# In the layer-norm feeds, GpSimd adds the mean row to every second k-tile

## The chip, the cores and the metric

The kernel runs on one core of a Trainium2 chip. The metric is device time in microseconds (us), the median of several runs. TensorE multiplies matrices, VectorE and ScalarE work element by element, GpSimd is a further elementwise engine, and SyncE issues the DMAs. All of them read and write SBUF; TensorE writes its results into PSUM banks, of which there are eight, each with a row of 512 float32 in each of 128 partitions.

## The reference, cut to what matters

The kernel computes a transformer-like model of three blocks over 512 tokens of 1024 features. What matters here is the layer norm and its place:

```
def layer_norm(t, g, b):
    mu = tf.mean(-1, keepdims=True)
    var = jnp.square(tf - mu).mean(-1, keepdims=True)
    return ((tf - mu) * lax.rsqrt(var + EPS) * g + b)

x = layer_norm(ALPHA * x + m[:, 2] * y, ...)
x = layer_norm(ALPHA * x + m[:, 5] * conv_glu_ffn(modulate(x, ...), *ffn, rows, GRID_W), ...)
u = silu(layer_norm(u, ln_g, ln_b))      # inside the conformer, ahead of u @ w2
```

Each of these results is the input of a matrix product.

## The kernel before, in words

Activations lie with the features in the partitions: a tensor of 1024 features by 512 tokens is `DT` = 8 k-tiles of 128 x 512 float32. A product over the features keeps its accuracy by splitting both operands into a rounded high part (type fp32r) and the low rest; `three_passes` (L245) then issues three matmuls, high by high, low by high and high by low, for each k-tile and output tile.

The kernel is a row of stages. Within a stage each engine runs its own list of instructions in order, and semaphores order the engines among each other; between two stages all engines meet. A stage that begins with a layer norm has a *feed*, an object of the class `LayerFeed` (L456). There are four: at the start of the first feed-forward block (tiles `ffn_x`), of the conformer's gate (`conf_x`), of the conformer's output product (`conf_in`), and of the second feed-forward block (`ffn_x` again). The mean times the inverse deviation, negated, is one row per token, spread over all partitions; so is the inverse deviation itself. In three feeds `closing` has left both in PSUM, the deviation in bank 6 and the mean in bank 7. In the `conf_in` feed both lie in SBUF (`stats`).

For k-tile k a feed does this:

- scale: VectorE multiplies `x[k]` by the row of inverse deviations (L481)
- center: VectorE adds the mean row (L472)
- form and high: ScalarE applies gain, bias and function twice, into `form`, a buffer of two tiles (L495), and into the high part (L497)
- low: VectorE subtracts the high part from `form` (L477)
- products: TensorE runs six matmuls on the k-tile (L248 to L250), three for each of two output tiles whose weights are already there.

VectorE's order is scale(k), center(k-1), low(k-2). ScalarE may form tile k only when low(k-2) is done, since `form` has two tiles. TensorE waits for low(k). While the feed begins, TensorE runs a few products on constants whose results nobody reads (`fill`, L256). Behind the feed each engine goes on in its list: ScalarE and VectorE split the next weights (L1048 and L1111, L1307 and L1367, L743 and L790 by stage), and SyncE fetches further weights when a slot has been split.

In these stages GpSimd only clears the borders of the convolution's buffer (L1015, L1246); in the `conf_in` stage it has nothing to do. `core.mean` is a row of 128 x 512 in SBUF which `closing` uses for a running sum, and which is free while a feed runs.

Of the kernel before, what the change touches and what calls it, by code (L numbers as in the profile page):

```python
# [11 lines left out]
ALU = mybir.AluOpType  # L12
ACT = mybir.ActivationFunctionType
# [4 lines left out]
DT = D // P  # L18
# [437 lines left out]
class LayerFeed:  # L456
# [3 lines left out]

    def __init__(self, core, x, parts, form, scale, bias, func=ACT.Identity, stats=None):
        self.rstd, self.mean = stats or (core.banks[6][:, :], core.banks[7][:, :])
        self.x, self.parts, self.form, self.scale, self.bias, self.func = x, parts, form, scale, bias, func

    names = ["scaled", "centered", "formed", "fed_high", "fed"]

    def dve(self, dve, scaled, centered, formed, fed_high, fed):
        x, form = self.x, self.form

        def center(k):  # L470
            dve.wait_ge(scaled, k + 1)
            dve.tensor_tensor(x[:, k, :], x[:, k, :], self.mean, ALU.add).then_inc(centered, 1)  # L472

        def low(k):
            dve.wait_ge(formed, k + 1)
            dve.wait_ge(fed_high, k + 1)
            dve.tensor_tensor(self.parts[1][:, k, :], form[:, k % 2, :], self.parts[0][:, k, :].bitcast(F32), ALU.subtract)\  # L477
               .then_inc(fed, 1)

        for k in range(DT):  # L480
            dve.tensor_tensor(x[:, k, :], x[:, k, :], self.rstd, ALU.mult).then_inc(scaled, 1)  # L481
            if k >= 1:
                center(k - 1)
            if k >= 2:
                low(k - 2)
        center(DT - 1)
        low(DT - 2)
        low(DT - 1)

    def act(self, act, scaled, centered, formed, fed_high, fed):  # L490
        for k in range(DT):
            act.wait_ge(centered, k + 1)
            if k >= 2:
                act.wait_ge(fed, k - 1)
            act.activation(self.form[:, k % 2, :], self.x[:, k, :], self.func, scale=self.scale(k), bias=self.bias(k))\  # L495
               .then_inc(formed, 1)
            act.activation(self.parts[0][:, k, :], self.x[:, k, :], self.func, scale=self.scale(k), bias=self.bias(k))\  # L497
               .then_inc(fed_high, 1)


class RootFeed:
# [6 lines left out]
    names = ["formed", "fed_high", "fed"]  # L508
# [22 lines left out]
class PlainFeed:  # L531
# [5 lines left out]
    names = ["fed_high", "fed"]  # L537
# [11 lines left out]
def closing(core, name, weights, acts, x, gate=None, center=True, eps=EPS, ahead=0, nxt=None, source=None, feed=None, rest=None, sq=None, lead=None,  # L549
# [27 lines left out]
    for t, k0, k1, prepared in bounds:  # L577
        if prepared:
            units.append((t, k0, k1, None))
        else:  # L580
# [7 lines left out]
    names = ["piece_in0", "piece_in1", "piece_high", "piece_low", "used", "taken", "r_done", "squared", "first_sum", "shift_done",  # L588
             "shifted", "body_sums", "last_sums", "counted", "var_done", "root_done", "inverted", "eps_in", "x_in",
             "x_ready", "next_in", "next_high", "summed_up", "squares_up"]  # L590
# [6 lines left out]
    with core.room(**rows) as (ring, shift, stat, eps_col, *own), \  # L597
            core.split_room(**{f"{name}_w": [P, slots - ready, per, P]}) as (own_w,), core.stage(*names) as (block, *sems):
        high, low = [[w_ready[n] for w_ready in (lead.ready if lead else ())] + [own_w[n][:, i] for i in range(slots - ready)]
                     for n in range(2)]  # L600
# [5 lines left out]
        feed_sems = extra[:len(feed.names)] if feed else []  # L606
# [6 lines left out]
        @block.sync  # L613
        def _(sp):
            def fetch(n):
                t, k0, k1 = pieces[n]
                if n >= 2 + ready:
                    sp.wait_ge(piece_low, n - 1 - ready)
                sp.dma_start(ring[:, n % 2, 0:k1 - k0], w[:, k0:k1, t * P:(t + 1) * P]).then_inc(piece_in[n % 2], 16)

            fetch(ready)
            fetch(ready + 1)
            if source is not None and not lead:
                sp.dma_start(x[:], source).then_inc(x_in, 16)
            for n in range(ready + 2, len(pieces)):
                fetch(n)
                if n == ready + 3 and lead:
                    sp.wait_ge(lead.fed_in(lead_sems), DT)
                    sp.dma_start(x[:], source).then_inc(x_in, 16)
                if n == ready + 3 and nxt is not None:  # L630
                    for slot in range(2):
                        sp.dma_start(core.pre_ring[:, slot], nxt[slot]).then_inc(next_in, 16)

        if lead:
            @block.gpsimd
# [255 lines left out]
class LastPair:  # L891


    names = ["value_in", "late_tapped0", "late_tapped1", "late_active", "late_products", "late_high", "late_low"]
# [66 lines left out]
def glu_ffn(core, name, w_up, gate_at, value_at, w_down, make_feed, x, renew, width, interior, taps, middle, conv_w, conv_b, func,  # L961
# [14 lines left out]
    with core.split_room(**{f"{name}_h": [P, FT, SEQ]}) as (h,), \  # L976
            core.room(**{f"{name}_pad": [P, 2, width], f"{name}_acc": [P, 2, SEQ], f"{name}_val": [P, 2, SEQ],
                         f"{name}_lit": [P, 2, SEQ]}) as (pad, acc, val, lit):
        with core.split_room(**{f"{name}_x": [P, DT, SEQ], f"{name}_w": [P, 2, DT, P]}) as (parts, (high, low)):
            feed = make_feed(parts, lit)  # L980
            names = ["slab_in0", "slab_in1", "high_done", "low_done", "tile_done", "banks_free", "bordered", "padded", "tapped0",
                     "tapped1", "active", "products", "h_high", "h_low", "slots_refilled", "next_in", "next_high"]
            with core.stage(*names, *feed.names) as (block, *sems):
                (slab_in0, slab_in1, high_done, low_done, tile_done, banks_free, bordered, padded, tapped0, tapped1, active,
                 products, h_high, h_low, slots_refilled, next_in, next_high, *feed_sems) = sems
                fed = feed_sems[-1]
# [11 lines left out]
                @block.sync  # L998
                def _(sp):
                    for u in range(2, 4):  # L1000
                        sp.dma_start(ring[:, u % 2], w[:, :, bass.ds(slab_at(0, u), P)]).then_inc(slab_in[u % 2], 16)
                    with sp.Fori(1, steps) as i:
                        for u in range(4):
                            feature = sp.snap(slab_at(i, u))
                            sp.wait_ge(low_done, 4 * i + u - 1)
                            sp.sem_inc(slots_refilled, 1)
                            sp.dma_start(ring[:, u % 2], w[:, :, bass.ds(feature, P)]).then_inc(slab_in[u % 2], 16)
                    for u in range(2):
                        sp.wait_ge(low_done, 4 * steps + u - 1)
                        sp.dma_start(ring[:, u], down[:, DT * u:DT * (u + 1), 0:P]).then_inc(next_in, 16)  # L1010

                @block.gpsimd
                def _(pool):
                    for j in range(2):
                        pool.memset(pad[:, j, :], 0.0).then_inc(bordered, 1)  # L1015

# [163 lines left out]
def conformer_gate(core, w1, w2, x, renew, make_feed, conv):  # L1180
# [24 lines left out]
    def theirs(j):  # L1205
# [3 lines left out]
    names = ["slab_in0", "slab_in1", "high_done", "low_done", "tile_done", "border", "banks_free", "gated", "begun",  # L1209
             "tapped", "diag_done", "pe_tapped", "added", "first_sum", "shift_done", "r_done", "squared", "mean_sum",  # L1210
             "summed", "mean_done", "square_done", "var_done", "root_done", "inverted", "eps_in", "next_in", "next_high"]
    with core.split_room(conf_x=[P, DT, SEQ], conf_w=[P, 2, DT, P]) as (parts, (high, low)), \
# [3 lines left out]
        with core.stage(*names, *feed.names) as (block, *sems):  # L1216
# [17 lines left out]
            @block.sync  # L1234
            def _(sp):
                for s in range(2, 2 * DT):
                    if s >= 4:
                        sp.wait_ge(low_done, s - 1)
                    sp.dma_start(ring[:, s % 2], slab(s)).then_inc(slab_in[s % 2], 16)
                for u in range(2):  # L1240
                    sp.wait_ge(low_done, 2 * DT)
                    sp.dma_start(ring[:, u], out[:, :, u * P:(u + 1) * P]).then_inc(next_in, 16)

            @block.gpsimd
            def _(pool):
                pool.memset(pad[:], 0.0).then_inc(border, 1)  # L1246

            @block.tensor
# [329 lines left out]
class Folds:  # L1578
# [8 lines left out]
    def pool(self, pool, scaled, folded):  # L1587
        core, mods = self.core, self.mods
        for n, (layer, part) in enumerate(((0, 3), (1, 0), (1, 3))):
            shift, scale = [mods[layer][:, (part + e) * DT:(part + e + 1) * DT, 0] for e in range(2)]  # L1590
            gain, bias = [core.cols_sb[:, COL_AT[name] + n:COL_AT[name] + 4 * DT:4] for name in ("post_ln_g", "post_ln_b")]
            pool.tensor_tensor(core.fold_sb[:, 0, n, :], gain, scale, ALU.mult).then_inc(folded, 1)
            pool.tensor_tensor(core.fold_sb[:, 1, n, :], bias, scale, ALU.mult).then_inc(scaled, 1)
            pool.tensor_scalar(core.fold_sb[:, 2, n, :], gain, ALPHA, None, ALU.mult).then_inc(folded, 1)
            pool.tensor_scalar(core.fold_sb[:, 3, n, :], bias, ALPHA, None, ALU.mult).then_inc(folded, 1)
            pool.wait_ge(scaled, n + 1)
            pool.tensor_tensor(core.fold_sb[:, 1, n, :], core.fold_sb[:, 1, n, :], shift, ALU.add).then_inc(folded, 1)
        at = COL_AT["conf_b2"]
        out_gate = mods[1][:, 2 * DT:3 * DT, 0]
        pool.tensor_tensor(self.gated_bias[:, :], out_gate, core.cols_sb[:, at:at + DT], ALU.mult).then_inc(scaled, 1)  # L1600
        pool.wait_ge(scaled, 4)
        pool.wait_ge(folded, 12)
        pool.tensor_tensor(core.fold_sb[:, 3, 1, :], core.fold_sb[:, 3, 1, :], self.gated_bias[:, :], ALU.add).then_inc(folded, 1)
# [2729 lines left out]
```

## Time and profile before

| what | value |
|---|---|
| median of 3 runs | 2852.64 us (2845.04 to 2854.54) |
| the profiled execution's own time | 2843.07 us |
| its span in the profile | 2841.3 us |
| TensorE busy | 2636.8 us (93% of the span) |
| VectorE busy | 1650.8 us (58%) |
| ScalarE busy | 1088.6 us (38%) |
| GpSimd busy | 162.6 us (6%) |

The profile records one execution. Its own time is 1.8 us longer than the span, and 9.6 us (0.34%) below the median of the runs. A busy TensorE counts each matmul from its start to its modelled end, so consecutive ones overlap a little. In all rows, PE is TensorE, PEld its weight load, DVE VectorE, ACT ScalarE, POOL GpSimd and SP SyncE; times in a timeline are counted from the start of the span.

### The profile page before, as it was taken

How to read it: one execution, taken by the hardware profiler on the slowest of the kernel's cores; microseconds unless marked ns; L12 is line 12 of the kernel's file. 1: busy time of each engine (PE TensorE's matmuls, PEld its weight loads, DVE VectorE, ACT ScalarE, POOL GpSimd, SP SyncE). 2: the span in 40 equal slices, each digit the busy share in tenths (PEclk: the TensorE clock that was granted, in tenths of full speed). 3: DMA queues.
4: the chain of work that ended last, by engine and by line, in shares of the span. 5: the costliest groups of instructions: out<-in, count | busy, mean ns of one | idle time of the engine just before them, and what ended most of it. 6: DMA issues, size and time to landing. Idle time of an engine off the chain costs nothing. (4 is left out here: it accounts for less than half of the span.)

```text
span 2841.3 us, 41630 instructions
## 1 busy us (share of the span) xinstructions
PE 2636.8 (93%) x16068; PEld 2026.0 (71%) x16068; DVE 1650.8 (58%) x2601; ACT 1088.6 (38%) x1798; POOL 162.6 (6%) x170
## 2 busy tenths in 40 slices
PE   6978899988889999999997899999899998999998
PEld 3743588776668788877663688878578866788886
DVE  3436412267766588743898688853664577544432
ACT  3441210146563455422523365532321154355521
POOL 0005300013222000000000000000000000000000
PEclk9989999999999999999998999999999999999999
DMA  8734312211114133241120233342332001333232
GB/s 299 242 115 145 122 45 67 59 37 41 43 44 132 53 103 92 78 133 46 45 58 16 60 104 96 96 113 65 92 100 67 3 10 30 83 102 96 81 110 69
DMA packets 382116, 240.93 MB, mean 85 GB/s; under 512 B 7825, under 2 KB 353809, under 8 KB 381969
## 3 DMA queue, kind: packets, MB, share of 16 engines
q1 hardware_dynamic: 381968, 238.89, 28.7%
q8 instruction: 102, 1.67, 0.3%
q14 instruction: 46, 0.37, 0.0%
HBM read 236.24 MB, written 2.10 MB: 84 GB/s over the span
## 5 line engine op out<-in xcount | busy, mean ns | idle before, releaser
L1149 DVE SCALAR_TENSOR_TENSOR ffn_acc<-ffn_pad,cols_sb,ffn_acc 128x512 f32<-128x512 f32 x380 | 264.0, 749 | 32.7 <-ACT ffn_acc L1076 32.7
L248 PE MATMUL bank<-ffn_x_high,pre_high 128*128 128x512 f32 x528 | 210.9, 399 | 4.9 <-DVE ffn_x_low L477 3.3
L250 PE MATMUL bank<-ffn_x_high,pre_low 128*128 128x512 f32 x528 | 209.0, 396 | 0.0
L249 PE MATMUL bank<-ffn_x_low,pre_high 128*128 128x512 f32 x528 | 208.9, 396 | 0.0
L248 PE MATMUL bank<-ffn_x_high,ffn_w_high 128*128 128x512 f32 x528 | 205.5, 389 | 0.0
L250 PE MATMUL bank<-ffn_x_high,ffn_w_low 128*128 128x512 f32 x528 | 205.5, 389 | 0.0
L249 PE MATMUL bank<-ffn_x_low,ffn_w_high 128*128 128x512 f32 x528 | 205.4, 389 | 0.0
L248 PE MATMUL bank<-ffn_h_high,ffn_down_w_high 128*128 128x512 f32 x480 | 190.5, 397 | 0.7 <-DVE ffn_h_low L944 0.7
L249 PE MATMUL bank<-ffn_h_low,ffn_down_w_high 128*128 128x512 f32 x480 | 189.6, 395 | 0.0
L250 PE MATMUL bank<-ffn_h_high,ffn_down_w_low 128*128 128x512 f32 x480 | 188.6, 393 | 0.0
L743 ACT ACTIVATE ffn_down_w_high<-ffn_down_ring 128x1408 fp32r<-128x1408 f32 (+1 forms) x45 | 60.5, 1345 | 211.1 <-PE bank L250 176.9
L790 DVE TENSOR_TENSOR ffn_down_w_low<-ffn_down_ring,ffn_down_w_high 128x1408 fp32r<-128x1408 f32 (+1 forms) x45 | 71.2, 1581 | 111.2 <-ACT ffn_down_w_high L743 111.2
L1372 DVE SCALAR_TENSOR_TENSOR conf_u<-conf_pad,cols_sb,conf_u 128x512 f32<-128x512 f32 x162 | 121.8, 752 | 16.9 <-ACT conf_u L1339 11.7
L1111 DVE TENSOR_TENSOR pre_low<-pre_ring,pre_high 128x1024 fp32r<-128x1024 f32 x60 | 73.4, 1224 | 97.9 <-ACT pre_high L1048 97.2
L248 PEld LDWEIGHTS bank<-ffn_x_high,pre_high 128*128 128x128 f32 x528 | 99.2, 188 | 36.0 <-DVE ffn_x_low L477 12.4
L250 PEld LDWEIGHTS bank<-ffn_x_high,pre_low 128*128 128x128 f32 x528 | 99.2, 188 | 24.3
L249 PEld LDWEIGHTS bank<-ffn_x_low,pre_high 128*128 128x128 f32 x528 | 99.3, 188 | 23.5
L248 PEld LDWEIGHTS bank<-ffn_x_high,ffn_w_high 128*128 128x128 f32 x528 | 99.1, 188 | 20.8 <-DVE ffn_w_low L1111 0.2
L249 PEld LDWEIGHTS bank<-ffn_x_low,ffn_w_high 128*128 128x128 f32 x528 | 99.1, 188 | 20.7
L250 PEld LDWEIGHTS bank<-ffn_x_high,ffn_w_low 128*128 128x128 f32 x528 | 99.1, 188 | 20.6
L1111 DVE TENSOR_TENSOR ffn_w_low<-pre_ring,ffn_w_high 128x1024 fp32r<-128x1024 f32 x66 | 80.5, 1223 | 47.6 <-ACT ffn_w_high L1048 47.6
L248 PEld LDWEIGHTS bank<-ffn_h_high,ffn_down_w_high 128*128 128x128 f32 x480 | 90.2, 188 | 23.4 <-DVE ffn_h_low L944 1.5
(731 smaller groups left out, 6207.8 us busy)
## 6 DMA issues: line engine op xcount, KB each, us to landing
ada_ring<-in_ada_w SPq DMA_DIRECT2D x48, 1024.0 KB, 7.0
pre_ring<-in_ffn_w_up SPq DMA_DIRECT2D x88, 512.0 KB, 3.9
pre_ring<-in_ffn_w_in SPq DMA_DIRECT2D x44, 512.0 KB, 3.9
ffn_down_ring<-in_ffn_w_down SPq DMA_DIRECT2D x28, 704.0 KB, 4.7
pj_ring<-in_w_in SPq DMA_DIRECT2D x24, 512.0 KB, 3.9
ffn_down_ring<-in_ffn_w_out SPq DMA_DIRECT2D x14, 704.0 KB, 4.3
pre_ring<-in_conf_w SPq DMA_DIRECT2D x18, 512.0 KB, 5.0
f_ring<-in_mix_w_in SPq DMA_DIRECT2D x32, 256.0 KB, 3.2
```

Source lines behind the costliest of these rows:

```text
L248: pe.matmul(bank, weights[0], acts[0], start=start, stop=False)
L249: pe.matmul(bank, weights[0], acts[1], start=False, stop=False)
L250: return pe.matmul(bank, weights[1], acts[0], start=False, stop=stop)
L743: act.activation(high[n % slots][:, 0:k1 - k0], ring[:, n % 2, 0:k1 - k0], ACT.Copy).then_inc(piece_high, 1)
L790: dve.tensor_tensor(low[n % slots][:, 0:k1 - k0], ring[:, n % 2, 0:k1 - k0], high[n % slots][:, 0:k1 - k0].bitcast(F32), ALU.subtract).the ...
L1111: dve.tensor_tensor(slot(u)[1], ring[:, u % 2], slot(u)[0].bitcast(F32), ALU.subtract).then_inc(low_done, 1)
L1149: dve.scalar_tensor_tensor(out=dst, in0=src, scalar=conv_w(2 * i + j, n), in1=dst, op0=ALU.mult, op1=ALU.add).then_inc(tapped[j], 1)
L1372: dve.scalar_tensor_tensor(out=conv[:, j, :], in0=pad[:, j % pads, n:n + SEQ], scalar=core.col("conf_dw_w", j, n), in1=conv[:, j, :], op0= ...
```

## The change

The centering of the odd k-tiles goes from VectorE to GpSimd. GpSimd cannot read the mean row in its PSUM bank, so ScalarE first copies it into `core.mean`; in the `conf_in` feed, where the row is in SBUF, only the semaphore is raised. VectorE centers the even tiles with the SBUF row too. VectorE's order becomes scale(k), scale(k+1), center(k), low(k-2), low(k-1) for k = 0, 2, 4, 6.

```
+    def pool(self, pool, scaled, mean_in, centered, pool_centered, formed, fed_high, fed):
+        pool.wait_ge(mean_in, 1)
+        for k in range(1, DT, 2):
+            pool.wait_ge(scaled, k + 1)
+            pool.tensor_tensor(self.x[:, k, :], self.x[:, k, :], self.mean_sb[:, :], ALU.add).then_inc(pool_centered, 1)
...
         def center(k):
+            if k == 0:
+                dve.wait_ge(mean_in, 1)
             dve.wait_ge(scaled, k + 1)
-            dve.tensor_tensor(x[:, k, :], x[:, k, :], self.mean, ALU.add).then_inc(centered, 1)
+            dve.tensor_tensor(x[:, k, :], x[:, k, :], self.mean_sb[:, :], ALU.add).then_inc(centered, 1)
...
-        for k in range(DT):
-            dve.tensor_tensor(x[:, k, :], x[:, k, :], self.rstd, ALU.mult).then_inc(scaled, 1)
-            if k >= 1:
-                center(k - 1)
-            if k >= 2:
+        for k in range(0, DT, 2):
+            scale(k)
+            scale(k + 1)
+            center(k)
+            if k:
                 low(k - 2)
-        center(DT - 1)
+                low(k - 1)
         low(DT - 2)
         low(DT - 1)
...
+        if self.own_mean is None:
+            act.activation(self.mean_sb[:, :], self.mean, ACT.Copy).then_inc(mean_in, 1)
+        else:
+            act.sem_inc(mean_in, 1)
         for k in range(DT):
-            act.wait_ge(centered, k + 1)
+            act.wait_ge(pool_centered if self.by_pool(k) else centered, k // 2 + 1)
```

In the stages, GpSimd's list gets `feed.pool(pool, *feed_sems)` ahead of the clearing of the borders (L1015, L1246), and in `closing` with a centered feed it gets a list with this alone.

## Rows read from the trace of the kernel before

**Rows 1.** Windows, conf_x and conf_in: busy PE, PEld, DVE, ACT, POOL; PEclk; DMA.

```profile
1340.80:1358.90 18.10, 15.64 (x55) 9.52 (x55) 16.15 (x27) 14.30 (x20) 1.46 (x1) 1.00 0.22 59
1549.40:1567.50 18.10, 15.34 (x52) 10.20 (x52) 16.11 (x27) 15.14 (x19) 0.00 (x0) 0.91 0.22 58
```

**Rows 2.** Timeline (start, duration, instruction, count, [idle <-releaser]), VectorE, conf_x feed.

```profile
1340.97 1.29 DVE L481 TENSOR_TENSOR x_sb<-x_sb,bank 128x512 f32<-128x512 f32 x2
...
1344.52 0.69 DVE L477 TENSOR_TENSOR conf_x_low<-conf_sq,conf_x_high 128x512 fp32r<-128x512 f32 x1 [0.47 <-ACT conf_x_high L497]
...
1348.12 0.69 DVE L477 TENSOR_TENSOR conf_x_low<-conf_sq,conf_x_high 128x512 fp32r<-128x512 f32 x1
...
1356.67 0.69 DVE L477 TENSOR_TENSOR conf_x_low<-conf_sq,conf_x_high 128x512 fp32r<-128x512 f32 x1 [0.72 <-ACT conf_x_high L497]
```

**Rows 3.** Timeline of ScalarE in the conf_x feed and behind it.

```profile
1342.89 0.81 ACT L495 ACTIVATE conf_sq<-x_sb,fold_sb 128x512 f32<-128x512 f32 x1 [5.34 <-DVE x_sb L472]
1343.61 0.80 ACT L497 ACTIVATE conf_x_high<-x_sb,fold_sb 128x512 fp32r<-128x512 f32 x1
...
1355.77 0.80 ACT L497 ACTIVATE conf_x_high<-x_sb,fold_sb 128x512 fp32r<-128x512 f32 x1
...
1368.65 0.81 ACT L1339 ACTIVATE conf_u<-conf_pad,cols_sb 128x512 f32<-128x512 f32 x1
```

**Rows 4.** Timeline of TensorE in the conf_x feed, up to the next tile.

```profile
1340.84 2.81 PE L256 MATMUL bank<-const_sb 128*128 128x512 f32 x6 [0.98 <-PEq L226]
...
1345.26 0.50 PE L248 MATMUL bank<-conf_x_high,pre_high 128*128 128x512 f32 x1 [1.61 <-DVE conf_x_low L477]
...
1357.50 0.41 PE L248 MATMUL bank<-conf_x_high,pre_high 128*128 128x512 f32 x1
...
1358.89 0.44 PE L248 MATMUL bank<-conf_x_high,conf_w_high 128*128 128x512 f32 x1
```

**Rows 5.** Timelines of the two ffn_x feeds: VectorE's first, TensorE in the last k-tile.

```profile
955.79 1.28 DVE L481 TENSOR_TENSOR x_sb<-x_sb,bank 128x512 f32<-128x512 f32 x2 [3.01 <-PEq L226]
...
972.58 0.50 PE L248 MATMUL bank<-ffn_x_high,pre_high 128*128 128x512 f32 x1
...
1620.56 1.28 DVE L481 TENSOR_TENSOR x_sb<-x_sb,bank 128x512 f32<-128x512 f32 x2 [2.99 <-PEq L226]
...
1637.10 0.40 PE L248 MATMUL bank<-ffn_x_high,pre_high 128*128 128x512 f32 x1
```

**Rows 6.** Timeline of the conf_in feed and what follows it.

```profile
1549.56 1.29 DVE L481 TENSOR_TENSOR conf_u<-conf_u,rstd 128x512 f32<-128x512 f32 x2
...
1565.32 0.69 DVE L477 TENSOR_TENSOR conf_in_low<-conf_form,conf_in_high 128x512 fp32r<-128x512 f32 x1 [0.72 <-ACT conf_in_high L497]
...
1567.45 1.51 SPq L619 DMA_DIRECT2D conf_out_ring<-in_conf_w  x2
...
1571.67 1.06 ACT L743 ACTIVATE conf_out_w_high<-conf_out_ring 128x1024 fp32r<-128x1024 f32 x1 [4.55 <-DMA conf_out_ring<-in_conf_w]
```

**Rows 7.** Timelines of GpSimd and VectorE in an earlier stage, from 844.9 us.

```profile
844.98 1.30 POOL L3022 TENSOR_TENSOR o_hg<-o_hg,o_gates 128x512 f32<-128x512 f32 x1 [35.53 <-ACT br_o_sq L3055]
...
845.46 1.37 DVE L3076 TENSOR_TENSOR y_low<-x_sb,y_high 128x512 fp32r<-128x512 f32 x1 [1.55 <-ACT y_high L3053]
...
846.24 1.74 POOL L3022 TENSOR_TENSOR o_hg<-o_hg,o_gates 128x512 f32<-128x512 f32 x1
...
846.75 1.78 DVE L3076 TENSOR_TENSOR y_low<-x_sb,y_high 128x512 fp32r<-128x512 f32 x1
```

**Rows 8.** Timelines of VectorE and GpSimd from 225 us.

```profile
225.23 2.48 DVE L2184 TENSOR_TENSOR xbc<-xbc,bank 128x512 f32<-128x512 f32 x4
...
226.13 1.90 POOL L2010 TENSOR_TENSOR ssd_xd<-x_tok,share 128x1024 f32<-128x1024 f32 x1
```

**Rows 9.** Groups by form, ScalarE (xcount | busy us, mean ns | idle before).

```profile
L1089 ACT ACTIVATE ffn_val<-bank 128x512 f32<-128x512 f32 x63 | 37.7, 599 | 155.5 <-PE bank L250 155.5
```

**Rows 10.** Timeline of TensorE in the conf_in feed, a matmul at the lower clock.

```profile
1556.70 0.63 PE L250 MATMUL bank<-conf_in_high,pre_low 128*128 128x512 f32 x1
```

More of the change, by code:

```diff
@@ L462, in __init__, with by_pool, dve, scale @@
         self.rstd, self.mean = stats or (core.banks[6][:, :], core.banks[7][:, :])
+        self.own_mean, self.mean_sb = stats, core.mean
         self.x, self.parts, self.form, self.scale, self.bias, self.func = x, parts, form, scale, bias, func
-    names = ["scaled", "centered", "formed", "fed_high", "fed"]
-    def dve(self, dve, scaled, centered, formed, fed_high, fed):
+    names = ["scaled", "mean_in", "centered", "pool_centered", "formed", "fed_high", "fed"]
+    def by_pool(self, k):
+        return k % 2 == 1
+    def pool(self, pool, scaled, mean_in, centered, pool_centered, formed, fed_high, fed):
[3 more added lines that the diff above has]
+            pool.tensor_tensor(self.x[:, k, :], self.x[:, k, :], self.mean_sb[:, :], ALU.add).then_inc(pool_centered, 1)
+    def dve(self, dve, scaled, mean_in, centered, pool_centered, formed, fed_high, fed):
         x, form = self.x, self.form
+        def scale(k):
+            dve.tensor_tensor(x[:, k, :], x[:, k, :], self.rstd, ALU.mult).then_inc(scaled, 1)
         def center(k):
+            if k == 0:
+                dve.wait_ge(mean_in, 1)
             dve.wait_ge(scaled, k + 1)
-            dve.tensor_tensor(x[:, k, :], x[:, k, :], self.mean, ALU.add).then_inc(centered, 1)
+            dve.tensor_tensor(x[:, k, :], x[:, k, :], self.mean_sb[:, :], ALU.add).then_inc(centered, 1)
         def low(k):
@@ L478, in low, with act @@
                .then_inc(fed, 1)
-        for k in range(DT):
-            dve.tensor_tensor(x[:, k, :], x[:, k, :], self.rstd, ALU.mult).then_inc(scaled, 1)
-            if k >= 1:
-                center(k - 1)
-            if k >= 2:
+        for k in range(0, DT, 2):
[3 more added lines that the diff above has]
+            if k:
                 low(k - 2)
-        center(DT - 1)
+                low(k - 1)
         low(DT - 2)
         low(DT - 1)
-    def act(self, act, scaled, centered, formed, fed_high, fed):
+    def act(self, act, scaled, mean_in, centered, pool_centered, formed, fed_high, fed):
+        if self.own_mean is None:
+            act.activation(self.mean_sb[:, :], self.mean, ACT.Copy).then_inc(mean_in, 1)
+        else:
+            act.sem_inc(mean_in, 1)
         for k in range(DT):
-            act.wait_ge(centered, k + 1)
+            act.wait_ge(pool_centered if self.by_pool(k) else centered, k // 2 + 1)
             if k >= 2:
@@ L632, in _ @@
                         sp.dma_start(core.pre_ring[:, slot], nxt[slot]).then_inc(next_in, 16)
+        if feed and center:
+            @block.gpsimd
+            def _(pool):
+                feed.pool(pool, *feed_sems)
         if lead:
@@ L1013, in _ @@
                 def _(pool):
+                    if renew is not None:
+                        feed.pool(pool, *feed_sems)
                     for j in range(2):
@@ L1245, in _ @@
             def _(pool):
+                feed.pool(pool, *feed_sems)
                 pool.memset(pad[:], 0.0).then_inc(border, 1)
```

## The prediction

> **What bounds the kernel now.** I read the busy shares first: TensorE is busy for 93% of the span and GpSimd for 6%, so GpSimd has room and only what TensorE waits for counts. The windows over the feeds come next [rows 1]: in 18.1 us of each, VectorE is busy for 16.1 us, ScalarE for 14.3 and 15.1, TensorE for 15.6 and 15.3 with its overlapping ends and its fills. Then the timelines tell who waits for whom. In the conf_x feed VectorE starts at 1340.97 [rows 2], and I count from there. Two scales take 1.29 us, so starts are 0.60 apart and one operation lasts 0.69. low(0) starts at 3.55, low(2) at 7.15: 1.80 us per k-tile, three operations of VectorE back to back. ScalarE begins to form at 1.92, its starts are 0.72 apart, and the last high ends at 15.60 [rows 3]. TensorE's fills are over at 2.68; its first product waits 1.61 us for low(0) and starts at 4.29, and the last k-tile's first product starts at 16.53 [rows 4]. Its six matmuls take 1.39 us, since the next product begins at 1358.89 [rows 4]; I use 1.40. So VectorE's 1.80 sets the pace, ScalarE's 1.43 and TensorE's 1.40 would be next. The feed is a fill of the pipeline: what it loses is lost for good, as long as the stage behind it has no slack. The ffn_x feeds have the same pattern, with the last k-tile's product at 16.79 and 16.54 after VectorE's start [rows 5]; the last low of conf_in ends at 16.45 [rows 6].
>
> **What is removed and what it would be worth.** Each feed takes 4 of 24 operations from VectorE. At 0.60 that is 2.40 us, 9.6 us in all. This holds only if VectorE's other operations keep their duration while GpSimd works.
>
> **What GpSimd does to VectorE.** The earlier stage has the same pair of operations side by side [rows 7]. GpSimd's first add runs alone in 1.30 us and ends at 846.28. VectorE's subtraction of two SBUF tiles starts at 845.46 and takes 1.37 instead of 0.69: it ends at 846.83, 0.55 after GpSimd's. GpSimd's next, started at 846.24, ends at 847.98, 1.15 after VectorE's. VectorE's next ends at 848.53, again 0.55 after. They alternate, each held until the other is through. An operation of VectorE with one input in PSUM is not held: four took 2.48 us in all, 0.68 each, although GpSimd ran a two-input operation through the last two [rows 8]. So I take from rows 7: GpSimd 1.30 alone, its end 1.14 after VectorE's where VectorE was first, VectorE's end 0.55 after GpSimd's where GpSimd was first. Scales out of PSUM run free; centers and lows, both now with two SBUF inputs, are held. The bounds are no hold at all and, above, this alternation.
>
> The Trainium skill says the same of the mechanism (SBUF — State Buffer, "SBUF: two separate sides"): the pair of ports that VectorE and GpSimd share is taken for a whole instruction, by whoever starts first, against a VectorE operation with two SBUF inputs. By its words a held operation would then need its whole 0.69 us, 1.99 in place of the 1.85 of the rows; the sum below would be near 7 us. The trace has 0.55, not 0.69, and I go by the trace.
>
> **The new order, step by step (three feeds with PSUM rows).** Times are from VectorE's start.
> - The copy of the mean row is priced at 0.60 like an eviction of this shape out of PSUM [rows 9]; ScalarE is idle for over 5 us before its first form [rows 3]. VectorE needs the row at 1.20. Cost 0. Without that cover it would be 0.6 per feed, 1.8.
> - scale(0) 0.00, scale(1) 0.60 to 1.29, center(0) 1.20 to 1.89. GpSimd could start on tile 1 at 1.33, is held by center(0), and ends at 3.03.
> - scale(2) 1.80, scale(3) 2.40 to 3.09, center(2) 3.00 to 3.69. GpSimd's tile 3 is held again and ends at 4.83.
> - low(0) could start at 3.60 (ScalarE's high(0) ends at 3.44). It is the loser now: it ends at 4.83 + 0.55 = 5.37, before 4.24. low(1) ends at 5.97.
> - The pair then repeats: scale, scale, center (3 x 0.60), a held low (1.77 less an overlap of 0.08), a free low (0.60): 4.09 us for two k-tiles, where before it was 3.60. low(2) ends at 9.46, low(4) at 13.55, low(5) at 14.15.
> - Tail. ScalarE's form(6) waits for low(4) as before for its buffer: form and high of 6 and 7 start 0.71 apart from 13.61, high(7) ends at 16.54, low(7) at 17.33. Before, 15.60 and 16.39: +0.95 on ScalarE and VectorE.
> - TensorE: first product at 5.42; from low(4) on it is the bound, four k-tiles of 1.40 behind 13.60: the last one's first product at 17.80.
>
> The same steps laid on the old order give 4.27 for the first product, 16.42 for the last k-tile's and 15.59 for the last high; the trace has 4.29, 16.53 and 15.60, so the method holds to 0.1 us.
>
> **Each feed.** In the ffn stages TensorE goes on without a pause, so its delay counts: 17.80 against 16.79 and 16.54 [rows 5], +1.0 and +1.3. In the conformer's gate the next thing is ScalarE's own list, through diagonals, sigmoid and renewal to conf_u at 1368.65, which VectorE's taps wait for [rows 3]: +0.95. In conf_in the row of deviations is in SBUF as well, so scale(2) is held by GpSimd: it ends at 3.57 instead of 2.49, and everything behind is 1.09 later. low(7) ends at 18.42 against 16.45: +2.0. What follows is VectorE's split of the first piece, which releases SyncE's next fetch (1567.45), which ScalarE waits for until 1571.67 [rows 6]; the delay goes through whole. Sum: 1.0 + 0.95 + 2.0 + 1.3 = +5.3 us.
>
> Border clearing moves behind GpSimd's four adds, to about 13 us after the start; it is wanted behind the feed, 7 us later. Cost 0 without a hold from GpSimd's clearing on VectorE's last lows; with one, one low would be later by at most the clearing's 1.46 us in conf_x [rows 1], and by less in the ffn feeds, where it is cut in two.
>
> **Rivals.**
> - *No hold in these stages.* The rows that show the hold [rows 7] are of an earlier stage; no feed has one yet, since GpSimd reads nothing there now. Then low(4) comes early enough that the ring of two forms and ScalarE set the pace: by the same steps high(7) would end at 14.03 and the last k-tile's product start at 15.3. Against the same steps on the old order that is -1.1 for each ffn feed and -1.6 for each of the others: -5.4, 2837.7 on the profiled execution, 2847.2 on the median. The full 9.6 (2843.0) would need ScalarE and TensorE to have no limit of their own; they have 1.43 and 1.40 per k-tile.
> - *TensorE's clock falls in the feeds.* This is the slower side. TensorE's idle time ahead of the first product grows from 1.61 to 2.7 us [rows 4], and by 2.2 us in conf_in. In conf_in the granted clock is already 0.91 over the window [rows 1]: for a part of it TensorE ran at 1.2 GHz instead of 2.4, a matmul 0.63 us instead of 0.40 [rows 10]. 0.09 of 18.1 us is 1.6 us of work, which is what such a stretch costs where TensorE is the bound. If it lies on the first two k-tiles, the gap ahead of low(2) (8.22 to 9.51) takes most of it up. One that is not covered in each of four feeds would give +6.4 more: 2864. It decides (over 0.3%) from three uncovered stretches on.
> - *The hold is real but falls less often.* GpSimd may start a little later than I take, and low(0) win against tile 3. This saves up to 1.1 per feed once: about +1 to +3, 2854 to 2856.
>
> **How the numbers follow.** The profiled execution took 2843.07 us; +5.3 makes 2848.4. The median of the runs is 9.6 us above it, and I add the same to it: 2852.64 + 5.3 = 2858. A change of 0.3% is 8.6 us, about what a measurement of this kernel can tell from none. Chances: the alternation as worked out, 0.55; held less often, 0.20; no hold, 0.08 (-0.19%, inside the 0.3%); the full gain of VectorE's time, 0.03; clock stretches or further waits, 0.14. The cases up to +8.6 us hold most of it: faster 0.05, same 0.81, slower 0.14. The range runs from no hold, 2847, to the alternation with four uncovered clock stretches and a little more, 2866.
>
> **What would show it.** GpSimd has four adds of about 1.7 us in each feed; low(0), low(2) and low(4) last about 1.77 us, low(1) and low(3) 0.69; scales out of PSUM stay at 0.68; low(2) to low(4) is 4.1 us; TensorE's first product moves to 5.4. Wrong if lows of 0.69 us lie beside GpSimd's adds, or if the feeds in ffn end earlier than 16.5. The prediction also falls if the stages behind the feeds give the delay back.

## The result, and the profile after

The changed kernel took 2860.74 us in the median of 20 runs (2852.06 to 2873.29), the kernel before 2851.86 us (20 runs, 2844.76 to 2856.05). The ratio is 1.0031 (95% interval 1.0022 to 1.0040): slower by 8.9 us, at the edge of the 0.3%. The forecast was 2858.0, which is +5.3 us. The profiled execution of the changed kernel took 2857.86 us and has a span of 2855.7 us.

The windows over conf_x (up to the next tile's first product) and conf_in answer to [rows 1]. Columns are those of [rows 1].

```profile
1352.30:1371.60 19.30, 15.71 (x55) 11.21 (x56) 17.25 (x22) 14.98 (x23) 7.96 (x5) 0.91 0.20 55
1561.50:1580.10 18.60, 14.50 (x45) 9.89 (x46) 16.64 (x21) 13.89 (x19) 6.55 (x4) 0.72 0.21 57
```

In conf_x the window has grown from 18.1 to 19.3 us. VectorE runs 22 instructions instead of 27 (four centers went to GpSimd, and a clearing of 0.06 us lies just outside the window) and is busy for 17.25 us instead of 16.15: fewer operations, more time. GpSimd's 7.96 us contain 1.46 of clearing. The granted clock is 0.91, where it was 1.00. The timeline of VectorE in this feed shows the longer operations (columns as in [rows 2]).

```profile
1352.32 1.28 DVE L481 TENSOR_TENSOR x_sb<-x_sb,bank 128x512 f32<-128x512 f32 x2
1353.52 0.68 DVE L487 TENSOR_TENSOR x_sb<-x_sb,mean 128x512 f32<-128x512 f32 x1
...
1355.92 2.36 DVE L492 TENSOR_TENSOR conf_x_low<-conf_sq,conf_x_high 128x512 fp32r<-128x512 f32 x2
...
1360.01 2.37 DVE L492 TENSOR_TENSOR conf_x_low<-conf_sq,conf_x_high 128x512 fp32r<-128x512 f32 x2
...
1364.10 2.37 DVE L492 TENSOR_TENSOR conf_x_low<-conf_sq,conf_x_high 128x512 fp32r<-128x512 f32 x2
...
1369.00 0.69 DVE L492 TENSOR_TENSOR conf_x_low<-conf_sq,conf_x_high 128x512 fp32r<-128x512 f32 x1 [0.72 <-ACT conf_x_high L516]
```

Two lows in a row take 2.36 us where two free operations take 1.28. The same view with a narrow window has the two of the first pair one by one:

```profile
1355.92 1.76 DVE L492 TENSOR_TENSOR conf_x_low<-conf_sq,conf_x_high 128x512 fp32r<-128x512 f32 x1
1357.61 0.68 DVE L492 TENSOR_TENSOR conf_x_low<-conf_sq,conf_x_high 128x512 fp32r<-128x512 f32 x1
```

All of the hold is in the first. GpSimd's timeline in the same feed tells what held it: the second of its first two adds ends at 1353.76 + 3.38 = 1357.14, and the low at 1357.68, 0.54 behind it.

```profile
1353.76 3.38 POOL L475 TENSOR_TENSOR x_sb<-x_sb,mean 128x512 f32<-128x512 f32 x2 [373.39 <-DVE x_sb L481]
1359.56 1.66 POOL L475 TENSOR_TENSOR x_sb<-x_sb,mean 128x512 f32<-128x512 f32 x1 [2.42 <-DVE x_sb L481]
1363.65 1.67 POOL L475 TENSOR_TENSOR x_sb<-x_sb,mean 128x512 f32<-128x512 f32 x1 [2.43 <-DVE x_sb L481]
1365.25 1.46 POOL L1273 MEMSET conf_pad<- 128x1626 f32 x1
```

TensorE's timeline there answers to [rows 4]: its first product waits 2.73 us instead of 1.61, and starts 5.42 us after VectorE's first operation instead of 4.29. It runs at the lower clock (0.63 us a matmul) until 1361.26 and at full clock from there on. It reaches the third k-tile at 1362.17, after low(2) has ended (1361.77), so there it waits no more; it still waits 0.86 us for low(4).

```profile
1357.74 0.74 PE L248 MATMUL bank<-conf_x_high,pre_high 128*128 128x512 f32 x1 [2.73 <-DVE conf_x_low L492]
1358.28 0.63 PE L249 MATMUL bank<-conf_x_low,pre_high 128*128 128x512 f32 x1
...
1365.92 0.50 PE L248 MATMUL bank<-conf_x_high,pre_high 128*128 128x512 f32 x1 [0.86 <-DVE conf_x_low L492]
...
1371.49 0.39 PE L248 MATMUL bank<-conf_x_high,conf_w_high 128*128 128x512 f32 x1
```

In conf_in, VectorE's timeline has one more hold, ahead of the first low. The row of deviations lies in SBUF, and scale(2) and scale(3) take 2.36 us together; the last low ends at 1580.03, 18.5 after the start, against 16.4 [rows 6].

```profile
1563.37 2.36 DVE L481 TENSOR_TENSOR conf_u<-conf_u,rstd 128x512 f32<-128x512 f32 x2
...
1566.26 2.35 DVE L492 TENSOR_TENSOR conf_in_low<-conf_form,conf_in_high 128x512 fp32r<-128x512 f32 x2
...
1579.34 0.69 DVE L492 TENSOR_TENSOR conf_in_low<-conf_form,conf_in_high 128x512 fp32r<-128x512 f32 x1 [0.72 <-ACT conf_in_high L516]
```

**Where the time went in the profiled executions.** Both traces hold the same instructions outside the feeds, so the same instruction can be looked up in both. The table has how much later each landmark lies in the changed kernel, in us.

| landmark | before | later by | added since the line above |
|---|---|---|---|
| first scale of the first ffn feed | 955.79 | 10.40 | |
| weight split behind it | 979.9 | 11.39 | +1.0 (forecast +1.0) |
| first scale of conf_x | 1340.97 | 11.35 | |
| first weight split behind it | 1358.7 | 12.33 | +0.98 (forecast +0.95) |
| first scale of conf_in | 1549.56 | 12.00 | -0.3 |
| splits behind it | 1586.9 | 14.13 | +2.13 (forecast +2.0) |
| first scale of the second ffn feed | 1620.56 | 14.14 | |
| weight splits some 60 us behind it | 1686.8 | 15.50 | +1.36 (forecast +1.3) |
| last normalization of that block | 1998.2 | 16.19 | +0.7 |
| beginning of the next stage | 2010.7 | 14.70 | -1.5 |
| own time of the execution | 2843.07 | 14.79 | +0.1 |

The four feeds cost 1.0 + 1.0 + 2.1 + 1.4 = 5.5 us, and nothing behind them gives it back: the offset of 15.50 stays the same to 0.02 us for 180 us. What lies outside them is small and of both signs; the -1.5 is explained under experiments 9 and 10, the +0.7 and -0.3 are not. The 10.4 us ahead of the first feed are not the change's. The instructions there are the same; 7.9 of them come from one stretch in which TensorE had the lower clock, seen in the windows 775 to 795, changed kernel first and kernel before second:

```profile
775.00:795.00 20.00, 20.00 (x166) 16.79 (x167) 4.89 (x10) 10.82 (x32) 0.00 (x0) 0.57 0.05 14
```

```profile
775.00:795.00 20.00, 18.35 (x207) 16.48 (x202) 7.34 (x20) 13.74 (x36) 0.00 (x0) 0.91 0.11 29
```

Experiments 3, 4, 6, 7, 9, 10 and 11 have this stretch too and 1, 2, 5 and 8 have not, whatever their feeds; it is scatter, and the profiled execution of before, at 2843.07 us, was faster than any of the kernel's 101 measured runs.

### The profile page after: what moved, and what is told of

It reads as the page before. It is cut to its first block and busy times, and to the rows that moved or that the text cites. A ratio compares the mean times of both kernels' runs of the same rounds, so it can differ in the third digit from the quotient of the medians.

```text
span 2855.7 us, 41642 instructions
## 1 busy us (share of the span) xinstructions
PE 2645.2 (93%) x16068; PEld 2037.5 (71%) x16068; DVE 1653.9 (58%) x2585; ACT 1089.8 (38%) x1801; POOL 188.2 (7%) x186
## 3 DMA queue, kind: packets, MB, share of 16 engines
q8 instruction: 102, 1.67, 0.3%
```

## The experiments

Each diff is against the changed kernel. Times of feeds are counted from VectorE's first operation; "next tile" is the first product of the next output tile, which lay at 18.31 (ffn), 17.92 (conf_x) and 17.95 (second ffn) before and lies at 19.33, 19.17 and 19.32 in the changed kernel.

**1. The new order, with VectorE adding the row to all tiles.** The mean row still comes from SBUF.

```diff
-        for k in range(1, DT, 2):          # GpSimd
+        for k in ():
...
             center(k)
+            center(k + 1)
...
-            act.wait_ge(pool_centered if self.by_pool(k) else centered, k // 2 + 1)
+            act.wait_ge(centered, k + 1)
```

> The changed kernel with VectorE's new order and the copied row, but with the odd tiles centered by VectorE, too, so GpSimd adds nothing. Theory (the cost of the change is the hold between GpSimd and VectorE): no low lasts longer than 0.69 us; counted from VectorE's first scale, the lows 0, 2, 4 start at 4.8, 8.4, 12.0, the last high ends at 15.7 and the last k-tile's products end at 18.3 in all four feeds; with the conf_in feed ending 2.0 us earlier than in the changed kernel. In all -5 us against the changed kernel and +1 against the kernel before, ratio to before 1.0004. Rival (the new order or the SBUF row costs the time, not GpSimd): ends near 17.3 us for the last low as in the changed kernel, ratio 1.003.

Measured: 2850.03 us, ratio 0.9995 (0.9980 to 1.0010). VectorE's timeline has two lows in 1.29 us throughout, although both inputs are in SBUF:

```profile
1350.22 1.29 DVE L492 TENSOR_TENSOR conf_x_low<-conf_sq,conf_x_high 128x512 fp32r<-128x512 f32 x2
1353.82 1.29 DVE L492 TENSOR_TENSOR conf_x_low<-conf_sq,conf_x_high 128x512 fp32r<-128x512 f32 x2
```

high(7) ends at 15.72, low(7) at 16.52, the next tile starts at 18.46, 18.33 and 18.47. So neither the copy, nor the SBUF row, nor the order costs more than 0.15 to 0.5 us per feed; what costs is GpSimd's work.

**2. GpSimd with one input.** GpSimd multiplies the odd tiles by 1.0 instead of adding the row, so the mean is left out of them.

```diff
-            pool.tensor_tensor(self.x[:, k, :], self.x[:, k, :], self.mean_sb[:, :], ALU.add).then_inc(pool_centered, 1)
+            pool.tensor_scalar(self.x[:, k, :], self.x[:, k, :], 1.0, None, ALU.mult).then_inc(pool_centered, 1)
```

> The changed kernel, but GpSimd multiplies its tiles by 1.0 (one input from SBUF) in place of adding the mean row (two inputs); this leaves the mean out of the odd tiles. GpSimd's operation should take about as long, near 1.5 us. Theory (the hold falls on two-input operations of both engines): the lows last 0.69 us, start at 3.60, 4.95, 7.35, the last high ends at 14.0 and the last low at 14.8 after the first scale; ratio to before 0.998 (-5 us). Rival 1 (any GpSimd operation on SBUF holds VectorE's two-input ones): lows 0, 2, 4 last about 2 us and the last low ends at 17.5 or later; ratio 1.003. Rival 2 (the changed kernel's time comes from lower clocks of TensorE, not from the feeds): feeds shorter, but ratio still 1.002 or more.

Measured: 2849.69 us, ratio 0.9992 (0.9979 to 1.0004). low(7) ends at 15.70: earlier than with two inputs (17.38), later than without any hold (14.8 expected). Neither of the two expected times is met, and the timelines of GpSimd and VectorE say why:

```profile
959.57 3.58 POOL L475 TENSOR_SCALAR x_sb<-x_sb 128x512 f32<-128x512 f32 x2 [73.42 <-DVE x_sb L481]
965.04 1.87 POOL L475 TENSOR_SCALAR x_sb<-x_sb 128x512 f32<-128x512 f32 x1 [1.89 <-DVE x_sb L481]
```

```profile
961.72 1.09 DVE L492 TENSOR_TENSOR ffn_x_low<-ffn_lit,ffn_x_high 128x512 fp32r<-128x512 f32 x1
963.07 0.69 DVE L492 TENSOR_TENSOR ffn_x_low<-ffn_lit,ffn_x_high 128x512 fp32r<-128x512 f32 x1 [0.26 <-ACT ffn_x_high L516]
```

GpSimd's one-input operation delays low(0) by 0.40 us instead of 1.07, and low(0) ends at 962.81, while GpSimd works on to 963.15. So this is not the alternation of [rows 7], in which one operation waits for the end of the other. Without the second input most of the hold is gone, and a smaller delay is left, whose mechanism these runs don't show. The edit also puts another and longer instruction in the place of the add, so it is not shown that the number of inputs alone makes the difference.

**3. VectorE centers with the PSUM row.** Only GpSimd uses the copy.

```diff
-            dve.tensor_tensor(x[:, k, :], x[:, k, :], self.mean_sb[:, :], ALU.add).then_inc(centered, 1)
+            dve.tensor_tensor(x[:, k, :], x[:, k, :], self.mean, ALU.add).then_inc(centered, 1)
```

> The changed kernel, but VectorE's centers of the even tiles read the mean row in its PSUM bank; GpSimd's read the copy. Theory (only VectorE operations with two SBUF inputs and GpSimd's two-input ones hold each other): the centers no longer hold GpSimd, whose first add lasts 1.30 instead of 1.69; lows 0, 2, 4 last 1.37 instead of 1.77, the pair takes 3.7 us in place of 4.1; in the three feeds with PSUM rows the last high ends at 15.4 and the last low at 16.2, the last products at 18.1. conf_in is unchanged. In all -3.4 us against the changed kernel. Rival (VectorE is held with PSUM operands as well): no change in the feeds, 17.3.

A single execution, 2859.19 us, which gives no ratio. GpSimd's and VectorE's timelines in conf_x:

```profile
1351.37 1.28 POOL L475 TENSOR_TENSOR x_sb<-x_sb,mean 128x512 f32<-128x512 f32 x1 [373.29 <-DVE x_sb L481]
1353.10 1.27 POOL L475 TENSOR_TENSOR x_sb<-x_sb,mean 128x512 f32<-128x512 f32 x1 [0.44 <-DVE x_sb L481]
```

```profile
1353.53 1.38 DVE L492 TENSOR_TENSOR conf_x_low<-conf_sq,conf_x_high 128x512 fp32r<-128x512 f32 x1
```

GpSimd, which no center holds any more, takes its 1.28 us instead of 1.58 to 1.67; low(0) takes 1.38 instead of 1.76, and ends 0.54 after GpSimd's add (1354.91 against 1354.37). high(7) ends at 15.51, low(7) at 16.31. The alternation is thus a matter of where operands lie: of VectorE's three kinds of operation, only those with two inputs in SBUF take part. conf_in, where both rows are in SBUF in either case, stays as in the changed kernel: its last low ends at 18.48.

**4. The old order with GpSimd.** scale(k), center(k-1) for odd k, low(k-2).

```diff
-        for k in range(0, DT, 2):
+        for k in range(DT):
             scale(k)
-            scale(k + 1)
-            center(k)
-            if k:
+            if k % 2:
+                center(k - 1)
+            if k >= 2:
                 low(k - 2)
-                low(k - 1)
```

> The change with the order of the kernel before: scale(k), center(k-1) where VectorE has it, low(k-2). Theory: low(0) is no longer late (3.54 us), but each odd low is held (1.77 us), the pair takes 4.1 us and the last low ends at 17.6, the last products at 19.5, 0.3 us later than with the new order. Rival (low(0)'s lateness of 1.2 us is what the new order costs): the last low ends near 16.4.

A single execution, 2866.24 us. Now the odd lows take 1.77 us, low(0) is free at 3.55, and low(7) ends at 17.72; the next tile starts at 19.68. The hold follows whichever low meets GpSimd. In the three feeds with PSUM rows the order of the change is the better one by 0.35 to 0.42 us. In conf_in it is the worse one: there the last low ends at 17.76 in the old order and at 18.48 in the new one. In both orders scale(2) is held there. In the old one it ends just as low(0) can start (3.56); in the new one low(0) meets GpSimd's next add as well and starts at 4.70.

**5. More fills.** Three more products on constants ahead of each feed's first product, so that TensorE idles less; one of three such edits is shown.

```diff
-                    fill(pe, core, core.banks[4], 3)
+                    fill(pe, core, core.banks[4], 6 if renew is not None else 3)
```

> The changed kernel with more products on constants ahead of the feeds' first product: 6 fills instead of 3 in the two ffn stages and the conformer's gate, 5 instead of 2 in conf_in, so TensorE's idle time ahead of the first product falls from 2.7 us to under 0.3 in three feeds. Theory (the time of the change is the held lows; the clock's falls in the feeds lie on gaps and cost nothing): the stretches of the lower clock that begin 5 to 7 us after the first scale go away, the feeds' ends stay (last low 17.4, next tile 19.3), and the ratio to before stays at 1.003 (1.002 to 1.004). Rival (the lower clock is what brings the measured +8.9 us above the +5.3 of the feeds): ratio 1.0015 or less.

Measured: 2858.95 us, ratio 1.0025 (1.0012 to 1.0038). The granted clock over the first ffn feed and conf_x is 1.00, and the feeds end where they did (next tile at 19.32, 19.22 and 19.34).

```profile
961.50:980.80 19.30, 17.05 (x60) 10.96 (x60) 17.28 (x22) 14.99 (x21) 7.74 (x6) 1.00 0.20 55
1347.40:1366.70 19.30, 17.02 (x61) 11.08 (x62) 17.23 (x23) 14.97 (x22) 7.97 (x5) 1.00 0.20 55
```

So the lower clock in the changed kernel's feeds costs nothing: the gaps ahead of low(2) and low(4) take it up. conf_in agrees: the changed kernel has 10.2 us of the lower clock there, this one 3.4, and the last low ends at 18.48 and 18.47. The granted clock over whole runs says the same: its mean is 0.971 in the kernel before, 0.969 in the changed kernel and 0.971 again with the fills, while the mean time is 2859.2 us (changed, all runs) and 2858.2 us (fills). The limit of this is seen in experiment 6, where the stretch in the first feed lasted 6.8 us: the next tile started at 19.51 instead of 19.33.

**6. conf_in as before,** the other three feeds as changed.

```diff
     def by_pool(self, k):
-        return k % 2 == 1
+        return k % 2 == 1 and self.own_mean is None
...
```

The rest of the edit gives conf_in its old order back.

> The changed kernel with the conf_in feed as before the change (its own order, all centers on VectorE). Theory: that feed is back at a last low ending at 16.4, the time from its first scale to that of the second ffn feed is 71.0 us instead of 73.1, and the other three feeds stay at 17.4. Rival (the stage behind conf_in would have absorbed it): that time stays within 0.5 us of the changed kernel's 73.1.

A single execution, 2859.72 us. low(7) of conf_in ends at 16.46, and from conf_in's first scale to that of the next feed it is 70.75 us, against 73.14 in the changed kernel and 71.00 before. The other feeds stay at 17.4. The delay of conf_in, 2.0 us in the feed, does go through whole: 2.1 us against before between these two marks, 2.4 against this run.

**7. GpSimd for two tiles, where no low waits.** GpSimd takes tiles 2 and 5 alone, VectorE centers the others from PSUM, and VectorE's order is written out so that no low has to wait for GpSimd; conf_in is left to VectorE, in the order of experiment 8.

```diff
+    def pool_tiles(self):
+        return (2, 5) if self.own_mean is None else ()
...
+        "S0 S1 C0 S2 C1 S3 S4 L0 C3 L1 S5 L2 C4 S6 L3 C6 L4 S7 L5 C7 L6 L7"
```

> A version built on the hold: GpSimd centers only tiles 2 and 5 and only where the rows are in PSUM, VectorE's centers read the PSUM row, and VectorE's order places its scales and centers, which are not held, beside GpSimd's adds; conf_in is on VectorE alone, in a new order in which the scales and centers run further ahead of the lows. Theory: no low is held for more than 0.3 us; in the three feeds the last high ends at 13.8, the last low at 14.6, the last products at 16.1 after the first scale (before: 15.6, 16.4, 17.8); in conf_in 14.8, 15.6. In all about -5.5 us against the kernel before, ratio 0.998. Rival (the feeds' ends do not reach the end of the run): the same feeds, ratio 1.000.

Measured: 2849.43 us, ratio 0.9995 (0.9980 to 1.0009). All lows take 0.69 us, high(7) ends at 13.81 and low(7) at 14.61, 1.8 us earlier than before (2.1 in the first ffn feed). The engines still meet once: low(2) runs first, from 6.60 to 7.29, and GpSimd's second add takes 1.68 us instead of 1.27. That costs VectorE nothing, and the add ends at 8.44, before ScalarE begins with tile 5 at 9.36. But the next tile starts at 17.81, 17.57 and 17.81, and not at 16.1. TensorE's timeline:

```profile
965.56 0.50 PE L248 MATMUL bank<-ffn_x_high,pre_high 128*128 128x512 f32 x1 [2.30 <-DVE ffn_x_low L502]
...
966.26 0.63 PE L250 MATMUL bank<-ffn_x_high,pre_low 128*128 128x512 f32 x1
...
978.43 0.40 PE L248 MATMUL bank<-ffn_x_high,ffn_w_high 128*128 128x512 f32 x1
```

TensorE idled 2.30 us, then had the lower clock for 3.4 us, and in this order no gap follows that could take it up. With the feed shorter, TensorE is the bound, and each of its losses counts.

**8. The same without GpSimd.** VectorE alone, in a written-out order with the centers earlier.

```diff
+        "S0 S1 C0 S2 C1 S3 S4 C2 L0 C3 L1 S5 C4 L2 S6 L3 C5 L4 C6 S7 L5 C7 L6 L7"
```

> No GpSimd and no copy of the row: VectorE does all 24 operations of each feed as in the kernel before, in the order S0 S1 C0 S2 C1 S3 S4 C2 L0 C3 L1 S5 C4 L2 S6 L3 C5 L4 C6 S7 L5 C7 L6 L7 (S scale, C center, L low). Theory (VectorE's idle time at the end of the feed, where only ScalarE's forms of tiles 6 and 7 are left, can be taken out by keeping VectorE ahead): last high at 14.8, last low at 15.6, last products at 17.1 in all four feeds, -3 us against the kernel before, ratio 0.999. Rival (the order is worth nothing): last low at 16.4.

Measured: 2851.05 us, ratio 1.0001 (0.9990 to 1.0012). low(7) ends at 15.64, the next tile starts at 18.25, 18.14 and 18.30, again behind 3.4 us of lower clock.

**9 and 10. Both with more fills.** Experiment 7 with two and experiment 8 with three more fills than the changed kernel has (and three more in `closing`, as in experiment 5; experiment 9's edit is shown).

```diff
-                fill(pe, core, total, 2)
+                fill(pe, core, total, 5 if center else 2)
...
-                    fill(pe, core, core.banks[4], 3)
+                    fill(pe, core, core.banks[4], 5 if renew is not None else 3)
```

> The version with tiles 2 and 5 on GpSimd, with 5 fills instead of 3 ahead of the first product in the ffn and gate feeds and 5 instead of 2 in conf_in. In that version the lows ended as worked out (14.6) but TensorE went on to the next tile at 17.8 and not at 16.1, with a stretch of the lower clock from 5.3 to 8.7 us in each feed. Theory (TensorE is the bound there, so such a stretch is no longer covered, and idle time ahead of the first product brings it): with the fills no such stretch begins in the ffn feeds and the gate, the next tile starts at 16.2 to 16.3, 1.6 us before the kernel before, and the ratio to before is 0.998. Rival (TensorE's lateness is something else, its pace with VectorE's new order): the next tile stays at 17.8 and the ratio at 0.9995.

> The same for the version with all on VectorE in the new order, with 6 fills in the ffn and gate feeds and 5 in conf_in. Theory: next tile at 17.1 instead of 18.2 (before: 17.9), ratio 0.999. Rival: 18.2 as without the fills.

Measured: experiment 9 2850.35 us, ratio 0.9995 (0.9983 to 1.0007); experiment 10 2850.42 us, ratio 0.9989 (0.9975 to 1.0002). In the feeds both did as forecast. In experiment 9 the first product waits 0.58 us, no lower clock follows, and the next tile starts at 16.27, 16.16 and 16.25, 1.7 to 2.0 us earlier than before; in experiment 10 at 17.19, 17.18 and 17.18.

```profile
967.23 0.50 PE L248 MATMUL bank<-ffn_x_high,pre_high 128*128 128x512 f32 x1 [0.58 <-DVE ffn_x_low L502]
...
978.57 0.40 PE L248 MATMUL bank<-ffn_x_high,ffn_w_high 128*128 128x512 f32 x1
```

The gain holds behind the first feed (the landmarks lie 6.5 us later than before's ahead of it, 4.6 behind it and through the whole block). Ahead of conf_x it shrinks by 1.5 us, in a place that the edit doesn't touch: the 16 small products that spread the statistics. TensorE's timeline there, experiment 9 first and the kernel before second:

```profile
1342.43 3.58 PE L711 MATMUL bank<-const_sb,ffn_down_stat 128*128 128x128 f32 x16 [0.50 <-DVE ffn_down_stat L912]
```

```profile
1337.82 2.05 PE L683 MATMUL bank<-const_sb,ffn_down_stat 128*128 128x128 f32 x16 [0.50 <-DVE ffn_down_stat L884]
```

The same happened to the kernel before at 2002.43, where these products took 3.53 us; the changed kernel took 2.05 there, the -1.5 in the table above. Such a stretch of the lower clock falls now here, now there. From the first feed to 1998 us experiment 9 gained 5.4 us on before in all, this loss included, about what the feeds were to give; from 2038 to 2450 us it lost it again in stages that hold no such feed. The other traces tell how much of such a loss is chance. Over the same stretch, from 2038 to 2450 us, the changed kernel gained 0.3 us on before in one execution and lost 2.6 in the other (experiment 11), experiment 8 gained 0.1, experiment 5 lost 4.9, and experiment 1, whose feeds take as long as before's to 0.5 us, lost 7.7. The one profiled execution of before was among the fastest there. But the runs do not bear out the gain either: the median of experiment 9 is 1.4 us below before's, where 5.7 was expected, and its interval, 0.9983 to 1.0007, includes no change at all and leaves out the expected 0.998. That the feeds' gain reaches the end of the run is not shown.

**11. The changed kernel once more,** beside experiments 9 and 10.

> The changed kernel beside these, unchanged. Its feeds repeat (last low 17.4, next tile 19.3; conf_in 18.5). Theory (the feeds are all that the change costs, and what was measured above +5.3 us is the scatter of TensorE's clock ahead of the first feed): ratio 1.002, and the time up to the first feed's first scale lies between 955 and 967 us as in the other kernels. Rival (the change costs more than its feeds): ratio 1.003 again, +8.5 us or more.

Measured: 2856.64 us, ratio 1.0010 (0.9998 to 1.0022), with the same feeds. This interval alone includes no change at all. Over all runs, the changed kernel has a mean of 2859.2 us (32 runs) and the kernel before 2851.7 (101 runs): 7.5 us slower, 0.26%, known to about 1.9 us either way.

## Why the prediction was right

**The hold** was the step that decided, and it is shown: with GpSimd's adds gone (1) no low takes over 0.69 us, with the PSUM row (3) the hold shrinks by 0.39 us, about what GpSimd's own hold was (0.37), in the old order (4) it moves to the odd lows. The two figures taken from [rows 7] carried over to another stage: VectorE ends 0.54 after GpSimd (0.55 used), and GpSimd's first add ends 1.15 after center(0) (1355.35 against 1354.20, 1.14 used).

**The times in the feed** were met to 0.1 us: low(0)'s end 5.36 (5.37 forecast), low(2) to low(4) 4.09 (4.09), high(7)'s end 16.57 (16.54), low(7)'s end 17.37 (17.33), TensorE's first product 5.42 (5.42), conf_in's last low 18.48 (18.42). The last k-tile's first product came at 17.92, 17.81 and 17.92 (17.80).

**The sum** was 5.3 us, and the four feeds show 5.5. Nothing behind the feeds gave the delay back. One sum beside it is too low: the prediction puts the feeds at near 7 us if a held operation needed its whole 0.69 us after the other's end. That reading would hold for GpSimd as well, whose held adds would need their whole 1.30 instead of 1.15. Three meetings a feed at 0.3 us make 3.6 more, near 9 us. That is close to the 8.9 of the first comparison, but by accident: the traces show 0.54 and 1.15 for the two ends, and 5.5 for the feeds.

**The zero costs** held. The copy of the mean row begins with the first scale and takes 0.60 us, and center(0) starts at 1.20 as forecast. GpSimd's clearing lies behind its adds, beside lows of 0.69 us.

**The median** is off by 2 to 3.6 us: 7.5 us over all runs or 8.9 in the first comparison, 5.3 forecast. The feeds account for 5.5. The rest is not attributed. It is no hidden cost of the clock in the feeds, since experiment 5 removes that and keeps its time. Two comparisons of the same two kernels gave 1.0031 and 1.0010, and the 7.5 over all runs is known to about 1.9, so a rest of 2 us is at the edge of the scatter: it may be chance or a small cost elsewhere. That the forecast of 2858.0 came within 2.7 us of the measured 2860.74 is thus partly luck; that the feeds came within 0.2 us is not.

**The rival of the clock** was half right. The longer idle time ahead of the first product did bring 3.4 us at the lower clock into every ffn and gate feed of the changed kernel, where before had none. That it would cost time was wrong here, for the reason the prediction gave: the gap ahead of low(2) takes up most of it, and the gap ahead of low(4) the rest. Experiments 7 and 8 show the same stretch without such a gap, and there it costs 1.0 to 1.6 us a feed (17.81 against 16.27, 18.25 against 17.19).

## What to carry to other kernels

Before giving GpSimd a part of VectorE's work, list for both engines which operations have two inputs in SBUF. Each meeting of two such operations cost VectorE 1.07 us here, more than the 0.60 us that the handed-over operation saved; in these feeds the handing-over shortened anything only where VectorE's operand lay in PSUM and the order let no low wait for GpSimd (experiments 7 and 9), and even there the whole run was not measurably faster. And a feed that fills a pipeline should be looked at on all engines: once VectorE was fast enough, TensorE's clock after the wait took the feed's gain, and fills gave it back in the feed.

## What the runs showed of the hardware

- A 128x512 VectorE operation with two SBUF inputs takes 0.69 us. When a GpSimd add of two SBUF inputs was there first, it ended 0.54 to 0.55 us after GpSimd's end. When VectorE was first, GpSimd's add ended 1.12 to 1.15 us after VectorE's end, instead of taking its free 1.27 to 1.30. With one of VectorE's inputs in PSUM neither was held (0.68 and 1.28, experiment 3).
- TensorE has no part in this: in all its rows it reads SBUF and writes a PSUM `bank`. (The opening of this document says of all engines that they write SBUF; for TensorE no row shows it.)
- A GpSimd multiply by a constant (one input, 128x512) took 1.79 to 1.87 us beside VectorE's operations, where an add of two inputs took 1.58 to 1.67. It lengthened a VectorE operation with two SBUF inputs from 0.69 to 1.09 us, without holding it until its own end.
- In the ffn and gate feeds TensorE was idle for 2.7 to 2.8 us ahead of its first product in the changed kernel, and a stretch at the lower clock followed each time (3.4 us, once 6.8 in experiment 6). With an idle time of 1.6 to 1.7 us (before, experiment 4) or under 0.6 us (the fills of experiments 5, 9 and 10) none followed there.
- Sixteen products of 128 columns took 2.05 us at the full clock and 3.53 to 3.58 at the lower one. The stretches at the lower clock move from run to run over the kernel: their sum was 145 us in the profiled execution of before and 162 to 196 us in the others, 176 and 193 in two executions of the changed kernel. The landmark at the first feed, ahead of which nothing was changed, lies 2 to 10 us later in the twelve other traces than in before's.
